# A three-block transformer step on one NeuronCore: moving the activations and the heads' tiles by 64 and 128 bytes in SBUF

## The reference

```python
h = jnp.square(jax.nn.relu(x @ w_ff1))   # 1,024 -> 4,096
x = x + h @ w_ff2                        # 4,096 -> 1,024
```

## Time and profile before

| | |
|---|---|
| median of three runs | 800.61 us (798.83 to 801.21) |
| the profiled execution | 799.77 us, of which the span of the profile is 798.0 |
| TensorE busy | 780.0 us (98%), 5,082 matmuls and as many weight loads |
| VectorE, ScalarE, GpSimd busy | 517.5, 411.7, 96.7 us |
| granted TensorE clock, mean over the span | 0.991 |

### The profile page before, as it was taken

The page is one execution under the profiler, slowest core; times in us unless marked ns, Lnnn a source line. Parts: engine busy times, 40 slices in busy tenths (PEclk is TensorE's granted clock), DMA queues, the critical chain, the costliest instruction groups (busy, mean ns, idle before and its releaser), DMA issues.

```text
span 798.0 us, 13073 instructions
## 1 busy us (share of the span) xinstructions
PE 780.0 (98%) x5082; PEld 684.4 (86%) x5082; DVE 517.5 (65%) x817; ACT 411.7 (52%) x613; POOL 96.7 (12%) x68
## 2 busy tenths in 40 slices
PE   9999999999999998999999899999999999999996
PEld 8998877799988886999787799889777999999995
DVE  6975547656665668377865775786766755555555
ACT  5534444554665443445665566565654544454441
POOL 2331000010100011111300307600000000000002
PEclk9999999999999998999999999999999999999999
DMA  9865544344863661676824354634217566556541
GB/s 336 314 211 173 197 159 129 99 162 108 252 203 135 202 199 67 196 228 185 261 97 131 119 167 152 211 106 143 95 57 228 192 216 207 182 189 210 175 142 53
DMA packets 76763, 137.43 MB, mean 172 GB/s; under 512 B 7072, under 2 KB 15520, under 8 KB 76704
## 3 DMA queue, kind: packets, MB, share of 16 engines
q1 hardware_dynamic: 75456, 132.15, 51.4%
q0 software_dynamic: 1248, 4.46, 1.7%
HBM read 132.80 MB, written 1.05 MB: 168 GB/s over the span
## 4 chain that ended last, share of the span: by engine, by line
PE 91%; DVE 4%; issue 2%; POOL 1%; ACT 1%; POOLq 0%; DVEq 0%; ACTq 0%
PE acc L1037 13%; PE acc L1039 13%; PE acc L1038 13%; PE acc L1045 12%; PE acc L1047 12%; PE acc L1046 12%; PE acc L1316 1%; PE acc L1350 1%; DVE w_lo L779 1%; PE acc L1193 1%; PE acc L1300 1%; PE acc L1289 1%; PE acc L1229 1%; PE acc L1185 1%; POOL v_lo L2354 1%
## 5 line engine op out<-in xcount | busy, mean ns | idle before, releaser
L779 DVE TENSOR_TENSOR w_lo<-raw,w_hi 128x1024 fp32r<-128x1024 f32 (+1 forms) x224 | 274.0, 1239 | 173.9 <-ACT w_hi L759 90.6
L1045 PE MATMUL acc<-x_hi,w_hi 128*128 128x256 f32 x840 | 236.7, 282 | 0.4 <-DVE x_lo L2137 0.4
L1047 PE MATMUL acc<-x_hi,w_lo 128*128 128x256 f32 x840 | 233.9, 278 | 0.0
L1046 PE MATMUL acc<-x_lo,w_hi 128*128 128x256 f32 x840 | 233.9, 278 | 0.0
L759 ACT ACTIVATE w_hi<-raw 128x1024 fp32r<-128x1024 f32 (+1 forms) x128 | 133.4, 1044 | 136.1 <-PE acc L1047 66.3
L749 ACT ACTIVATE w_hi<-raw 128x1024 fp32r<-128x1024 f32 x109 | 116.0, 1064 | 111.4 <-PE acc L1047 57.5
L1045 PEld LDWEIGHTS acc<-x_hi,w_hi 128*128 128x128 f32 x840 | 157.9, 188 | 3.3 <-issue 2.5
L1046 PEld LDWEIGHTS acc<-x_lo,w_hi 128*128 128x128 f32 x840 | 158.6, 189 | 0.8 <-issue 0.5
L1047 PEld LDWEIGHTS acc<-x_hi,w_lo 128*128 128x128 f32 x840 | 158.3, 189 | 0.0
L1037 PE MATMUL acc<-w_hi,cat_hi 128*128 128x512 f32 x272 | 108.9, 400 | 0.2 <-DVE w_lo L779 0.2
L1039 PE MATMUL acc<-w_hi,cat_lo 128*128 128x512 f32 x272 | 107.0, 393 | 0.0
(11 more groups left out here) (286 smaller groups left out, 917.7 us busy)
## 6 DMA issues: line engine op xcount, KB each, us to landing
raw<-in_w_ff SPq DMA_DIRECT2D x32, 1024.0 KB, 5.3
raw<-in_w_in_even SPq DMA_DIRECT2D x28, 1024.0 KB, 5.1
raw<-in_w_in_odd SPq DMA_DIRECT2D x16, 1024.0 KB, 5.6
raw<-in_w_in SPq DMA_DIRECT2D x16, 1024.0 KB, 5.6
raw<-in_w_out_even SPq DMA_DIRECT2D x12, 1024.0 KB, 5.8
raw<-in_w_out SPq DMA_DIRECT2D x4, 1024.0 KB, 5.0
raw<-in_w_in_even SPq DMA_DIRECT2D x4, 512.0 KB, 6.2
raw<-in_w_ukv_even SPq DMA_DIRECT2D x8, 256.0 KB, 3.3
```

What stands on the lines that cost most here:

```text
L779: ins = eng.tensor_tensor(lo, r, hi.bitcast(F32), ALU.subtract)
L1045: pe.matmul(o, wh[:, k, fs], hi[:, ka, :], start=start and f % 2 == 0, stop=False, skip_group_check=True)
L1046: pe.matmul(o, wh[:, k, fs], lo[:, ka, :], start=False, stop=False, skip_group_check=True)
L1047: ins = pe.matmul(o, wl[:, k, fs], hi[:, ka, :], start=False, stop=stop, skip_group_check=True)
```

## The change

Both gaps become 64 bytes smaller. Everything from `x_hi` to `cat_gap` moves down by 64 bytes, everything from `cat_hi` on by 128.

```diff
@@ -551,7 +551,7 @@
         w_hi = sb("w_hi", [P, 2, 2048], F32R)
         w_lo = sb("w_lo", [P, 2, 2048], F32R)
         res = sb("res", [P, T, D])
-        sb("x_gap", [P, 48])
+        sb("x_gap", [P, 32])
         x_hi = sb("x_hi", [P, KD, S], F32R)
         x_lo = sb("x_lo", [P, KD, S], F32R)
@@ -574,7 +574,7 @@
 
         soft = sb("soft", [P, PROBS, 2, 2])
 
-        sb("cat_gap", [P, 208])
+        sb("cat_gap", [P, 192])
         with nc.sbuf_tensor("cat_hi", [P, 24, S], F32R) as cat_hi, nc.sbuf_tensor("cat_lo", [P, 24, S], F32R) as cat_lo:
             pass
```

## The result

The changed kernel takes 813.25 us (median of four, 811.45 to 814.09) where the kernel before takes 800.91 in the same runs: a ratio of 1.0149, 95% interval 1.0123 to 1.0176. It is slower by 12.3 us. The forecast was 793.0 and faster, with a range up to 810, so both its sign and its range missed. The rival in which the 256-column products pay, at 811.0, came within 2.3 us.

The account below looks back on a forecast made before the run. The prediction held the kernel bound by TensorE's matmul steps, busy 780.0 of 798.0 us. Gains of 5.3 + 2.2 = 7.5 us took 799.77 to 792.3, or 793.0 on the median's scale; likeliest case 786 to 798, whole range up to 810.

Parts of the forecast that it names:

- The rival in which the 256-column products pay: Feature products: at 128 bytes each of 2,520 steps takes 120 ns as at distance 0, giving 811.0 us; chance 0.29.
- the no-effect rival: TensorE stretches: entry chooses the step, distance only shuffles entries, so time stays 798 to 803 us; chance 0.19.
- term (1): 2,520 feature products with x moving: 1,210 go from 117.7 to 113.3 ns, 5.3 us gained.
- Term (2): 936 token products with heads stationary: steps go to 226.7 ns, 2.2 us gained; loss bounded at 2.2 us.
- a step above 230: TensorE's timeline: a step in none of the rows, such as 220 ns or above 230, would mean wrong in kind.
- Term (3): 528 token products with x stationary: taken as nothing, bounded by 4.8 us gained and 1.2 us lost.

Follow-up runs that it names:

- e3: Kernel before with 960 bytes put in front of w_hi, both gaps as before, so x and heads' tiles stay at distance 192: 800.24 us, ratio 1.0007.
- e4: Kernel before with only w_hi, w_lo and res 64 bytes higher, x and heads' tiles at their old addresses, both distances 128: 812.78 us, ratio 1.0155.
- k1 to k5: Kernel before, first product split in two in four feature chunks, columns or chunks varied: 799.49, 799.65, 799.90, 796.17, 797.12 us in order.
- e1: Kernel before with only x moved, to distance 128 from the weights, heads' tiles left at 192: 809.52 us, ratio 1.0118.
- e2: Kernel before with only the heads' tiles moved, to distance 64 from the weights, x left at 192: 804.97 us, ratio 1.0058.

## Why the prediction was wrong

**Right:** that TensorE's steps are the whole matter, that no other engine and no wait enters, that a stretch has one of a few steps, and that the distance and not the place sets which are on offer. e3 and e4 show it from both sides. At 128, 160 and 224 bytes the steps lie closer together than the prediction's rows suggested (stretches of 117.3 to 120.0 ns).

The Trainium skill, page "TensorE: Matmul & The Clock Gate", section "Step-by-step: what each phase is for", speaks of two independent read ports, one for each operand. What the no-effect rival drew from it, that no distance could matter, doesn't hold for this form: moving the weights alone took the ratio to 1.0155, moving them with everything else left it at 1.0007.

**The step that failed** is the choice behind term (1), "I take the shorter step for (1) and 226.7 for (2), because the shorter step is already the one that half of the features fall into: it exists on these tiles, stays once entered, and a shift of one 64-byte unit has only to change which state the entries choose". That took the two steps for properties of the tiles. They are properties of the distance: at 128 the x features have 118.7 and 120.0 and no 113.3 at all. The entry does choose (the stretches from 159 and 320 us in k1 to k5), but only among the values that the distance offers. Instead of 5.3 us won, the term was 8.8 lost by the trace; e1, which has it together with the 1.4 us of the x tokens, measured 9.0 for both.

**Term (2)** failed in the same way. 226.7 was read at distance 0 and used at 64, which is not nearer to 0 in any sense that the runs bear out: 64 gives 233.3. I had bounded the loss by "the same 2.3 ns", and 4.1 was outside; e2 measured 4.4 us, of which 0.5 are the rank features, for which the sum had no term. The prediction named a step above 230 as a sign of being wrong in kind, "in none of these rows". It was in the trace of the kernel before, unread: at 497 us 48 token products with x stationary, at distance 192, take 7.00 us by 30, 233.3 ns, at a granted clock of 1.00.

```profile
498.66 0.40 PE L1039 MATMUL acc<-w_hi,x_lo 128*128 128x512 f32 x1
...
505.66 0.40 PE L1039 MATMUL acc<-w_hi,x_lo 128*128 128x512 f32 x1
```

So the 512-column products too have two steps at 192, 228.9 and 233.3, and the loss to reckon with was at least 4.4 ns.

**Term (3)** was costed at nothing and lost 1.4 us, 0.2 over its bound.

**The rival that came nearest** had the right place and sign, but its 811.0 is close by luck: 128 does not act as 0 does. Its features are at 119.0 and not 120, 8.8 us and not 11.6; its x tokens lose 2.7 ns where the rival gave them 2.3; and the heads' 3.8 us lost are not in it. The errors cancel. The evidence was there to be weighed: the one distance other than 192 that the old trace held was worse for 256 columns, and I put more chance on the side for which no row spoke. The range's upper end, 810, left out the case in which both streams lose.

## What to carry to other kernels

Where TensorE reads two float32r streams back to back, read the steps between the starts of successive matmuls, by form, and not the busy share. If they exceed the column count at the granted clock by more than a few nanoseconds, try the distance between the moving and the stationary buffers modulo 256 bytes: here the choice was worth up to 1.6% of the kernel, and the best distance differs between wide and narrow products. With a distance that offers two steps, look where long stretches begin; one product split in two at each of four entries brought 0.4%. Which entries, and how to split, was found by trying, and a stretch must be compared over several traces before its step is put down to an edit.

## What the runs showed that was not expected

- The step of a matmul depends on the distance of its two streams modulo 256 bytes: 0 and 256 gave the same 120.0 and 226.7 ns, 192 and 448 the same 113.3 or 117.8 and 229 or 233. What in the memory does this was not tested.
- At one and the same distance, 192, 256-column products have two stable steps, 113.3 and 117.8 ns, and 512-column products two, 228.9 and 233.3, each kept over hundreds of matmuls. A single product split in two moved a stretch of 288 features from one to the other in five kernels of five. Some stretches change without a split; why is open.
- Distances of 32, 160 and 224 bytes, off by half a 64-byte unit, put token products at 233 ns: above both neighbours at 224, no better than 64 at 32.
- With the heads' tokens at distance 0 (226.7 ns) the MLP's features behind them entered at the longer step, so the best distance of each form by itself did not make the best kernel (802.06 us against 799.79 in the same runs).
